# Latent attention: a second pair of rotary buffers, filled one head ahead, and a new order of its opening

## The reference

```python
proj = x @ w_in
cq, ckv, k_rope = split(proj, [384, 640])            # 384, 256 and 64 wide
cq, ckv = rms_norm(cq, q_norm), rms_norm(ckv, kv_norm)
q = (cq @ w_uq).reshape(b, s, 16, 128 + 64)
q_nope, q_rope = q[..., :128], q[..., 128:]
q_rope, k_rope = apply_rope(q_rope, cos, sin), apply_rope(k_rope, cos, sin)
w_uk, w_uv = w_ukv per head                          # 128 and 128 columns of each head
scores = (q_nope . (ckv @ w_uk) + q_rope . k_rope) * 192 ** -0.5
o = softmax(scores) @ (ckv @ w_uv)                   # per head
out = o.reshape(b, s, 2048) @ w_o
```

## Time and profile before

| | |
|---|---|
| Median of 3 runs | 2370.27 us |
| The profiled execution: its own time, its span | 2372.49 us, 2370.6 us |
| PE busy, 10372 matmul records | 2291.2 us (97%) |
| POOL, DVE, ACT busy | 1568.0, 1271.2, 648.5 us |
| Mean granted clock of TensorE | 0.989 of full speed |

### The profile page before, as it was taken

One profiled execution on the slowest core, in us unless ns is written; L12 is line 12 of the kernel. 1 busy time (PEld: TensorE's weight loads), 2 busy tenths in 40 slices (PEclk: granted clock), 3 DMA queues, 4 the chain that ended last, 5 costly groups with the idle time before them and its releaser, 6 DMA issues.

```text
span 2370.6 us, 27451 instructions
## 1 busy us (share of the span) xinstructions
PE 2291.2 (97%) x10372; PEld 1857.8 (78%) x10372; DVE 1271.2 (54%) x1820; ACT 648.5 (27%) x1190; POOL 1568.0 (66%) x1530
## 2 busy tenths in 40 slices
PE   7999989999999899999999999999999999999998
PEld 6888877888887677777778888878767787888886
DVE  6674727145245666256372454458875444626354
ACT  3343433101013345245231010132345232202112
POOL 7556556877776545544668777769425947878784
PEclk9999999999999899999999999999999999999999
DMA  5222222333332211211324333323212322333332
GB/s 162 76 71 80 72 79 73 112 97 97 98 98 76 59 35 36 71 42 32 97 73 128 98 99 111 98 76 116 71 37 80 111 67 89 96 97 97 98 96 73
DMA packets 110868, 200.13 MB, mean 84 GB/s; under 512 B 12305, under 2 KB 18705, under 8 KB 110737
## 3 DMA queue, kind: packets, MB, share of 16 engines
q1 hardware_dynamic: 107568, 194.72, 27.4%
q10 hardware_dynamic: 3168, 3.67, 0.5%
HBM read 196.24 MB, written 2.10 MB: 84 GB/s over the span
## 4 chain that ended last, share of the span: by engine, by line
PE 87%; DVE 6%; POOL 4%; ACT 2%; issue 1%; DMA 0%; SPq 0%; DVEq 0%; POOLq 0%
PE bank L469 26%; PE bank L471 25%; PE bank L470 25%; POOL wL L2612 2%; POOL wH L2610 1%; DVE bank L1834 1%; DVE h L1826 1%; PE bank L998 1%; PE bank L502 1%; PE bank L864 1%; DVE tmp L1826 1%; PE bank L869 1%; PE bank L870 1%; PE bank L865 1%; PE bank L866 1%
## 5 line engine op out<-in xcount | busy, mean ns | idle before, releaser
L2612 POOL TENSOR_TENSOR wL<-raw,wH 128x512 fp32r<-128x512 f32 (+2 forms) x731 | 1000.7, 1369 | 60.9
L2610 POOL TENSOR_SCALAR wH<-raw 128x512 fp32r<-128x512 f32 (+2 forms) x731 | 531.2, 727 | 616.4 <-PE bank L471 523.6
L469 PE MATMUL bank<-aH,wH 128*128 128x512 f32 x1376 | 547.0, 398 | 19.2 <-DVE aL L1834 9.6
L471 PE MATMUL bank<-aH,wL 128*128 128x512 f32 x1376 | 537.5, 391 | 0.0
L470 PE MATMUL bank<-aL,wH 128*128 128x512 f32 x1376 | 537.4, 391 | 0.0
L469 PE MATMUL bank<-uH,wH 128*128 128x512 f32 x960 | 375.7, 391 | 5.6 <-DVE uL L1826 5.6
L470 PE MATMUL bank<-uL,wH 128*128 128x512 f32 x960 | 374.5, 390 | 0.0
L471 PE MATMUL bank<-uH,wL 128*128 128x512 f32 x960 | 374.5, 390 | 0.0
L469 PEld LDWEIGHTS bank<-aH,wH 128*128 128x128 f32 x1376 | 258.9, 188 | 78.7 <-issue 13.1
L470 PEld LDWEIGHTS bank<-aL,wH 128*128 128x128 f32 x1376 | 259.0, 188 | 57.0 <-issue 4.1
L471 PEld LDWEIGHTS bank<-aH,wL 128*128 128x128 f32 x1376 | 258.9, 188 | 54.7
(11 more groups left out here) (315 smaller groups left out, 3202.3 us busy)
## 6 DMA issues: line engine op xcount, KB each, us to landing
raw<-in_ws SPq DMA_DIRECT2D x699, 256.0 KB, 2.6
raw<-in_ws SPq DMA_DIRECT2D x24, 192.0 KB, 2.3
h<-in_xT SPq DMA_DIRECT2D x4, 512.0 KB, 7.3
E<-in_memT ACTq DMA_DIRECT2D x16, 128.0 KB, 2.6
out<-c_F SPq DMA_DIRECT2D x8, 256.0 KB, 2.1
tmp<-in_pT ACTq DMA_DIRECT2D x4, 256.0 KB, 3.2
raw<-in_ws SPq DMA_DIRECT2D x8, 128.0 KB, 2.1
g_hc<-in_cst SPq DMA_DIRECT2D x1, 640.0 KB, 9.2
```

Source lines behind the costliest of these rows:

```text
L469: P.e.matmul(o, lH, rH, start=start, stop=False, skip_group_check=skip)
L471: return P.e.matmul(o, lL, rH, start=False, stop=stop, skip_group_check=skip)
L2610: G.e.tensor_scalar(H, x, 1.0, 0.0, MUL, ADD).then_inc(*G.did("wH", n))
L2612: G.e.tensor_tensor(L, x, H.bitcast(F32), SUB).then_inc(*G.did("w", n))
```

## The change

- There are two pairs of rotary buffers, `m_qr[j][i]`; heads 2p and 2p + 1 use pair p mod 2. So a pair can be filled while the other is read.
- In the loop, `rope_in` and the turning of the pair for heads hd + 3, hd + 4 stand in the odd head hd (up to 11); the split of it into `m_qr` (`rotated`, which was the end of `rotate`) stands in the even head after it. The pair of heads 2 and 3 goes in before `scores(0)`.
- The opening: the squares of `cq` go to `m_P[0]` instead of `sums` and `sq`, ahead of the `ckv` scale; PE's statistics matmul reads them from there; DVE makes the `ckv` tiles complete first, and the rotary key last; `values_in(0)` comes ahead of the two rotary key matmuls, `key_in(0)` behind `query_in(0)` and `rotate(0)`; the scores of head 0 are four groups of three matmuls and then four of two.
- Head 8 is begun within head 7: `heads_in(8)` stands between `turned(7)` and `values(7)`, `scores(8)` ahead of `mla_out(0)`. The keys of heads 8 and 9 are loaded apart, so there are 732 pieces.
- The places in the plan and of the divisions follow.

```diff
     def keys(hd):
-        add("mla_w_ukv", 0, (0, 1), ((256 * hd, 128), (256 * hd + 256, 128)))
+        if hd in (8, 9):
+            add("mla_w_ukv", 0, (0, 1), cols((256 * hd, 128)))
+        elif hd % 2 == 0:
+            add("mla_w_ukv", 0, (0, 1), ((256 * hd, 128), (256 * hd + 256, 128)))
...
         if hd % 8 == 7:
-            divided[len(out) + 1] = hd - 1
-            divided[len(out) + 5] = hd
-            mla_out(hd // 8)
+            divided[len(out) + (hd == 15)] = hd - 1
             if hd == 7:
                 head(8)
+            divided[len(out) + (5 if hd == 15 else 2)] = hd
+            mla_out(hd // 8)
...
-            m_qr = [sb(f"m_qr{i}", [128, T], FR, st) for i in range(2)]
+            m_qr = [[sb(f"m_qr{j}{i}", [128, T], FR, st) for i in range(2)] for j in range(2)]
...
-            stat_end("cq", tiles=3, tail=False, freed=(V, "cn", 2))
+            b = take("stat", "cq")
+            P.wait_ge(V, "sum", ("cq",))
+            P.e.matmul(b.ap[:, :], ones, m_P[0][:, 0, :], start=True, stop=True).then_inc(*P.did("stat", "cq"))
+            give(b, V, "cn", 2)
...
+                if hd == 0:
+                    bs = [take("ms", hd, n) for n in range(4)]
+                    for n in range(4):
+                        scores_nope(hd, n, bs[n])
+                    for n in range(4):
+                        scores_rope(hd, n, bs[n])
...
+            values_in(0)
             b1, b2 = take("kr1"), take("kr2")
...
-            values_in(0)
-            key_in(0)
             rope_in(0)
             query_in(0)
             rotate(0)
+            key_in(0)
+            rope_in(2)
             scores(0)
             for hd in range(16):
-                ahead, turn = hd % 8 != 7, hd % 2 == 0 and hd < 14
+                ahead, turn = hd % 8 != 7, hd % 2 == 1 and hd < 12
                 if ahead:
                     heads_in(hd + 1)
                 if turn:
-                    rope_in(hd + 2)
+                    rope_in(hd + 3)
                 turned(hd)
                 if ahead:
                     scores(hd + 1)
+                elif hd == 7:
+                    heads_in(8)
                 if turn:
-                    rotate(hd + 2)
+                    rotate(hd + 3)
+                elif hd == 0:
+                    rotate(2)
                 values(hd)
                 if hd == 7:
+                    scores(8)
                     mla_out(0)
-                    heads_in(8)
-                    scores(8)
...
+            def query_square(k):
+                A.wait_ge(V, "lat", k)
+                do(m_P[0][:, k, :], F[:, k, :], ACT.Square).then_inc(*A.did("sq", ("cq",), k))
...
-            def rotate(hd):
+            def rotated(hd):
                 A.wait_ge(V, "qr", hd)
-                if hd:
-                    A.wait_ge(P, "ms", hd - 1, 3)
+                if hd > 2:
+                    A.wait_ge(P, "ms", hd - 3, 3)
...
+            add_query_squares(1)
+            normed(3)
+            add_query_squares(2)
+            normed(4)
+            normed_low(3)
+            normed_low(4)
             V.wait_ge(P, "kr")
             tt(F[0:64, 5, :], bk("kr")[0:64, :], r[0:64, :], MUL).then_inc(*V.did("kr"))
...
                 if ahead:
                     scores(hd + 1)
+                elif hd == 7:
+                    heads_in(8)
                 if turn:
-                    rotate(hd + 2)
+                    rotate(hd + 3)
+                elif hd == 0:
+                    rotate(2)
+                elif hd % 2 == 0 and hd < 14:
+                    rotated(hd + 2)
                 values(hd)
+                if hd == 0:
+                    rotated(2)
```

More of the change, by code:

```diff
@@ L125, in plan @@
     values(0)
-    keys(0)
     rope(0)
     query(0)
+    keys(0)
+    rope(2)
     for hd in range(16):
@@ L856, in heads_in, with scores_nope, scores_rope @@
                 key_in(hd)
-            def scores(hd):
[L859 to L871, removed]
+            def scores_nope(hd, n, b):
+                c = cols128(n)
+                P.wait_ge(V, "qnL", hd)
+                P.wait_ge(V, "knL", hd)
+                P.e.matmul(b.ap[:, :], m_qnH[:, c], m_knH[:, :], start=True, stop=False)
+                P.e.matmul(b.ap[:, :], m_qnH[:, c], m_knL[:, :], start=False, stop=False)
+                P.e.matmul(b.ap[:, :], m_qnL[:, c], m_knH[:, :], start=False, stop=False)
+            def scores_rope(hd, n, b):
+                qr = m_qr[hd // 2 % 2][hd % 2][:, cols128(n)]
+                P.wait_ge(V, "qrL", hd // 2 * 2)
+                P.wait_ge(V, "krL")
+                P.e.matmul(b.ap[:, :], qr, m_krH[:, :], start=False, stop=False)
+                P.e.matmul(b.ap[:, :], qr, m_krL[:, :], start=False, stop=True).then_inc(*P.did("ms", hd, n))
+                give(b, A, "mp", hd, n)
+            def scores(hd):
+                if hd == 0:
[4 more added lines that the diff above has]
+                        scores_rope(hd, n, bs[n])
+                else:
+                    for n in range(4):
+                        b = take("ms", hd, n)
+                        scores_nope(hd, n, b)
+                        scores_rope(hd, n, b)
             def turned(hd):
@@ L1478, in latent @@
                 do(m_cH[:, k, :], tmp[k % 2][:, :], ACT.Copy).then_inc(*A.did("cH", k))
[L1480 to L1484, removed]
+            query_square(0)
+            query_square(1)
+            rstd(256, "ckv")
+            query_square(2)
+            latent(3)
+            latent(4)
             rstd(384, "cq")
@@ L1497, in values_in, with key_high @@
                     do(aVH[:, t, :], bk("mV", quad, t)[:, :], ACT.Copy).then_inc(*A.did("mVH", quad, t))
+            def key_high():
+                A.wait_ge(V, "kr3")
+                do(m_krH[:, :], F[:, 6, :], ACT.Copy).then_inc(*A.did("krH"))
             def rope_in(hd):
@@ L1549, in act @@
             values_in(0)
-            head_in(0, "kn", m_knH)
+            key_high()
             rope_in(0)
             head_in(0, "qn", m_qnH)
-            rotate(0)
-            A.also("rope done")
+            head_in(0, "kn", m_knH)
+            rotated(0)
             scores(0)
+            rope_in(2)
             for hd in range(16):
-                ahead, turn = hd % 8 != 7, hd % 2 == 0 and hd < 14
+                ahead, turn = hd % 8 != 7, hd % 2 == 1 and hd < 12
                 if ahead:
@@ L1564, in act @@
                     scores(hd + 1)
-                if turn:
-                    rotate(hd + 2)
+                elif hd == 7:
+                    heads_in(8)
+                if hd % 2 == 0 and 0 < hd < 14:
+                    rotated(hd + 2)
                 values(hd)
+                if hd == 0:
+                    rotated(2)
                 if hd == 7:
+                    scores(8)
                     A.wait_ge(V, "krL")
@@ L2271, in dve @@
             values_in(0)
-            head_in(0, "kn", m_knH, m_knL)
+            V.wait_ge(A, "krH")
+            low(m_krL[:, :], F[:, 6, :], m_krH[:, :]).then_inc(*V.did("krL"))
             head_in(0, "qn", m_qnH, m_qnL)
             rotate(0)
+            head_in(0, "kn", m_knH, m_knL)
+            rotated(0)
             scores(0)
             for hd in range(16):
-                ahead, turn = hd % 8 != 7, hd % 2 == 0 and hd < 14
+                ahead, turn = hd % 8 != 7, hd % 2 == 1 and hd < 12
                 if ahead:
```

82 lines of the change are left out of this document (43 added, 39 removed).

## The result

| | before | after |
|---|---|---|
| Median of the runs | 2370.43 us (2368.69 to 2372.69) | 2343.88 us (2342.45 to 2344.69) |
| Ratio, 95% interval | | 0.9887 (0.987 to 0.9904) |
| The profiled execution: time, span | 2372.49, 2370.6 us | 2344.64, 2342.8 us |
| Mean granted clock | 0.989 | 0.993 |

The change gives 26.6 us by the medians, 27.8 by the two spans. The forecast was 28.8 us and 2341.5; the time lies in the range.

A forecast was written before the change was run, and what follows sets the result against it. PE bounds the kernel, busy 97% of the span, so only its idle or half-clock time can be gained: 14.5 + 8.2 + 6.1 = 28.8 us off 2372.5 gives 2343.7, less 2.2 for the median, 2341.5; range 2338 to 2350.

The forecast's parts named there:

- Opening, 14.5 us: Last `kr` matmul to head 0's transposes: 40.4 us, 24.9 of it work; the other 15.5 recovered, less 1.0 new wait.
- the new wait ahead of the transposes: Opening, ahead of `turned(0)`: head 0's softmax would come late, an estimated 1.0 us of new PE wait.
- The seven waits, 8.2 us: Heads 2, 4 to 14: scores wait for the key's low part because of DVE's order; all 8.2 us go.
- Head 7, 6.1 us: Head 7, transposes to `mla_out(0)`: 10.5 us, 4.4 of it work; `rope_in(10)`, `heads_in(8)` and a swap cover the other 6.1.
- At nothing: The extra piece, the second pair of buffers and the moved divisions were counted as costing nothing.
- The rule against it: DVE's moved half subtractions could each wait out a POOL operation, 4.2 us for two; head 14 waits some 1.4: 2342.9.
- The first: Rival: the waits only change heads, odd heads' keys come as late, the 8.2 us stay: 2349.7; chance 0.11.
- The third: Rival: slower, DVE and ACT bound every head through held PSUM banks; 2374.5 at 2.2 us a head; chance 0.03.
- the fourth: Rival: the opening does not come earlier, another chain being as late; only 14.3 us left: 2356.0; chance 0.06.
- The second: Rival: the clock falls anyway in the opening or behind a short wait elsewhere: 2344.5 to 2346.5; chance 0.12.
- the prediction's own signs of being wrong: New wait over 1.5 us at `turned(0)`, odd-head waits for `m_knL`, a new half-clock stretch, or a longer later stage.

The follow-up runs named there:

- e2: Kernel after with only the opening changed; heads' loop and head 8 in the old order: median 2359.2 us.
- e7: Kernel after with the squares of `cq` in the old two buffers and DVE's old order of additions and low parts: median 2346.3 us.
- e6: Kernel after with the scores of head 0 in four groups of five matmuls, as all other heads have them: median 2343.8 us.
- e4: Kernel after with the half copies and half subtractions directly behind the turning, in the odd head: median 2349.6 us.
- e5: Kernel after with head 8's inputs and scores begun behind `mla_out(0)` again: median 2345.4 us.
- e3: Kernel after with one pair of rotary buffers in place of two: median 2342.9 us.
- e1: Kernel after again, no edit, a second execution with its own trace: median 2343.5 us.
- e8: Kernel after with two more float32 matmuls in the opening, so everything behind lies 1.72 us later: median 2344.2 us.
- e9: Kernel after with eight needless matmuls filling the 1.99 us wait ahead of differential attention's head 2 scores: median 2341.2 us.
- e10: Kernel after with that differential attention wait filled, plus plain float32 matmuls of constants in two more waits, at 321 and 773 us: median 2340.4 us.

## Why the prediction was right

*Opening, 14.5 us.* Measured from the n0 statistics to head 1's scores: 54.79 us before, 39.99 after, 14.8 less; 14.7 when done alone (e2). The way of counting, work by starts at full clock and all else as gain, held: the 92 matmuls and four float32 ones take 25.2 us from L822 to the transposes, where 24.9 were added up. The low parts of `ckv` took 1.86 us for the two instead of 1.51 each, and the new wait ahead of the transposes was 0.4 us instead of 1.0: the divisions' chain was mis-sized by 0.6 us. POOL did not stop splitting at 816.35 as taken over from before, but went on to 820.2, and one low part of `cq` took 1.32 us beside it; PE waited for none. Of the 14.8 us the squares of `cq` are worth 4.6 (e7) and the scores in two passes 1.0 (e6). The other 9 or so, from the values ahead of the rotary key and from the second rotary query ahead of the scores, were not taken apart.

*The seven waits, 8.2 us.* By starts 3.7 us at heads 2, 4 and 6, 1.7 at head 8 and 2.9 at the other three, 8.3 together. Six have the cause that was named, DVE's order: e4 puts the halves directly behind the turning again and gets waits wherever only the transposes cover the key. The seventh, at head 8, has another (e5): nothing stood between its key and its scores, and DVE's order has no part in it. The forecast laid all seven to one cause; that the sum was right all the same is luck, since the change also moves head 8. One reading was off: the prediction has the turning done 2.8 us before the low parts were begun, and by the earlier trace rows it is 3.5 us before `uL`, the row ahead of them (863.68 to 867.22), which was in its favour.

*Head 7, 6.1 us.* Measured 6.1 (10.52 us less 4.4). The step that named what covers it was wrong in its weights: with head 8 late only 0.4 us of that stall return (e5). DVE's rows of the half subtractions show why, before and then after:

```profile
958.73 2.53 DVE L1826 TENSOR_TENSOR m_qr<-tmp,m_qr 64x512 fp32r<-64x512 f32 x2 [1.41 <-ACT m_qr L1230]
```

```profile
936.77 2.62 DVE L1864 TENSOR_TENSOR m_qr<-tmp,m_qr 64x512 fp32r<-64x512 f32 x2 [0.99 <-ACT m_qr L1259]
```

They cost about the same and stand at the same place of DVE's program, but before they began 2.3 us behind the start of head 7's transposes (956.48), and now 1.8 us ahead of it (938.53), since the turning is no longer in front of them and `rope_in(10)` holds the transposes back by 2.1 us. e5 has both of these too, its halves begin 1.8 us ahead as well; no run parts the one from the other. Together that is 4.0 of the 4.6 us by which the low parts came behind the transposes' end. Moving head 8 is worth 2.05 us, 1.7 of them, by starts, the wait of its own scores, which the forecast had counted among the seven.

*At nothing.* The second pair costs and brings nothing (e3). The 732nd piece and the moved divisions were not run alone; in latent attention PE's list has one wait for POOL left, the 0.2 us at head 0.

*The rule against it.* A pair of DVE's half subtractions behind head 0 took 2.2 to 2.6 us, where before it took 1.4 to 2.5; one of them took 1.69 us at most, 1.68 before. No matmul waited for `m_qr` or for head 14's key. The 4.2 us for a pair, and with them the 1.4 us, that the Trainium skill (SBUF — State Buffer, on the engine side of its ports) would have allowed did not appear.

*The rivals.* The first fell: no wait at odd heads. The third and the fourth fell too: no head is slower, and the opening came 15 us earlier. The second came true outside the opening: behind the 1.99 us wait in differential attention the clock falls in some traces, which costs 3.15 us in that of the kernel after. So two of the prediction's own signs of being wrong were there, a new half-clock stretch and a later stage that is longer. The terms of the sum measured 14.8 + 8.3 + 6.1 = 29.2 us, yet the median is 2.4 us above the 2341.5. The argument against this rival was a misreading of before's trace, that the clock fell only behind idle stretches of 2.7 us or more. It fell there behind a shorter one too, for 3.4 us from 1614.4:

```profile
1614.73 0.80 PE L571 MATMUL bank<-aH,wH 128*128 128x512 f32 x1 [1.65 <-POOL wL L2612]
```

Against before's runs beside e1 the gain is 28.2 us. What part of a median is due to these stretches is not shown, since only one execution of each kernel was traced.

## What to carry to other kernels

Where one engine is the bound, count its work by the distance of starts at full clock between two of its instructions; what is left is the most that any reordering there can give, and here it was given almost whole. A wait's cause is found by asking what the releasing engine did just before and what the waiting one could have done: moving work that nobody needs yet (the halves) to a place where other matmuls cover it was worth more than doubling buffers, which gave nothing. A gain of 1% is to be read from the stage that was changed, since half-clock stretches in others move the total by 3 us.

## What the runs showed of the hardware

- The same wait of 1.99 us, at the same place of the program, is followed by no half clock (before, e5 to e8), by 3.4 us of it (e1) or by 6.8 (after, e2, e3, e4). What decides it is not shown.
- Shorter waits do it too: behind the one of 1.65 us near 1585 (1614 before) the clock falls for 3.4 us in ten of the twelve traces and not in e1 and e9, while behind one of 1.77 us at 1597 it stays up in the trace of before.
- A half-clock stretch cost about half its length where PE is the bound (1.5 to 1.8 us for 3.4, 3.15 for 6.8), and nothing at 773 us, where PE waits for DVE and POOL anyway (e10).
- Plain float32 matmuls of constants keep the clock at the 2.4 GHz level in a wait as well (e10: 1.00 instead of 0.66 at 317 us, behind 5.6 us without work in all other traces).
- After equal waits of 2.8 us the clock stayed low for 10.2 us (before) and for 3.4 us (e7).
